# VectorE's order around the first item, the last expert's gather and last chunk, and a weight place that holds three chunks

## What is computed

```
logits = xt @ w_router + b_router            # 256 x 32
top_val, top_idx = top_k(logits, 4); gate = softmax(top_val)
for each expert e, for the tokens that chose it:
    hdn = x @ w_mlp1[e] + b_mlp1[e]          # 1024 -> 2048
    glu = min(hdn[:, :1024], 7); lin = clip(hdn[:, 1024:], -7, 7)
    y   = (glu * sigmoid(1.702 * glu) * (lin + 1)) @ w_mlp2[e] + b_mlp2[e]
out = sum over a token's 4 experts of gate * y
```

## Time and profile before

| what | value |
|---|---|
| median of three runs | 1119.99 us (1119.98 to 1119.99) |
| the profiled execution, its own time | 1121.66 us |
| its span, first to last instruction | 1119.8 us |
| mean granted TensorE clock | 0.995 |
| TensorE matmul busy | 1073.4 us (96%) |
| VectorE / ScalarE busy | 382.2 us (34%) / 247.1 us (22%) |
| read from HBM | 437.67 MB, 392 GB/s over the span |

### The profile page before, as it was taken

One profiled execution on the slowest core, in us unless ns is written; L12 is line 12 of the kernel. 1 busy time (PEld: TensorE's weight loads), 2 busy tenths in 40 slices (PEclk: granted clock), 3 DMA queues, 4 the chain that ended last, 5 costly groups with the idle time before them and its releaser, 6 DMA issues.

```text
span 1119.8 us, 14338 instructions
## 1 busy us (share of the span) xinstructions
PE 1073.4 (96%) x5327; PEld 471.7 (42%) x5328; DVE 382.2 (34%) x852; ACT 247.1 (22%) x346; POOL 3.0 (0%) x12
## 2 busy tenths in 40 slices
PE   8999999999999999999889999999988889998996
PEld 8888888533333333333333333333333333332332
DVE  5987787422232222222222222222222222222223
ACT  5745674311111111110111111111111111111112
POOL 0000000000000000000000000000000000000000
PEclk9999999999999999999999999999999999999999
DMA  9755488999999999999999999999999999999996
GB/s 331 238 164 170 154 273 363 424 419 422 428 427 434 429 431 434 430 429 431 431 433 404 432 431 431 431 431 431 431 431 431 433 431 434 434 433 433 423 424 265
DMA packets 38309, 439.15 MB, mean 392 GB/s; under 512 B 5292, under 2 KB 5480, under 8 KB 22440
## 3 DMA queue, kind: packets, MB, share of 16 engines
q1 hardware_dynamic: 37776, 437.26, 93.2%
q10 hardware_dynamic: 504, 1.47, 0.5%
HBM read 437.67 MB, written 1.05 MB: 392 GB/s over the span
## 4 chain that ended last, share of the span: by engine, by line
PE 70%; DMA 26%; DVE 2%; ACT 2%; issue 0%; DVEq 0%; SPq 0%; PEldq 0%; ACTq 0%
PE bank L1162 29%; PE bank L1217 15%; DMA late_slots<-in_w_mlp_dram 14%; DMA ring<-in_w_mlp_dram 11%; PE bank L821 9%; PE bank L1064 4%; PE bank L815 2%; PE bank L1103 2%; PE bank L983 2%; PE bank L1031 2%; PE bank L1087 1%; ACT xn L716 1%; PE bank L1154 1%; DMA xs<-in_x_dram 1%; PE bank L1080 0%
## 5 line engine op out<-in xcount | busy, mean ns | idle before, releaser
L1162 PE MATMUL bank<-ring,xn 128*64 128x512 f32 x1232 | 280.0, 602 | 18.3 <-DMA ring<-in_w_mlp_dram 18.2
L1162 PE MATMUL bank<-late_slots,xn 128*64 128x512 f32 x880 | 197.9, 596 | 12.6 <-DMA late_slots<-in_w_mlp_dram 12.6
L1162 PEld LDWEIGHTS bank<-ring,xn 128*64 128x64 f32 x1232 | 85.1, 138 | 179.5 <-issue 152.4
L1217 PE MATMUL bank<-ring,smo 128*64 128x512 f32 x624 | 138.3, 595 | 0.0
L728 ACT ACTIVATE xn<-bank 128x512 f32<-128x512 f32 x33 | 19.7, 598 | 436.6 <-PE bank L1162 436.6
L1162 PEld LDWEIGHTS bank<-late_slots,xn 128*64 128x64 f32 x880 | 59.9, 136 | 126.6 <-issue 105.4
L1730 DVE SCALAR_TENSOR_TENSOR moe_y_lo<-bank,st,moe_y_hi 128x512 fp32r<-128x512 f32 x33 | 24.8, 751 | 235.5 <-ACT moe_y_hi L735 235.5
L1217 PE MATMUL bank<-late_slots,smo 128*64 128x512 f32 x416 | 92.1, 595 | 0.0
L1714 DVE TENSOR_SCALAR xn<-xn 128x512 f32<-128x512 f32 x33 | 14.1, 427 | 190.8 <-ACT xn L728 190.8
L1217 PEld LDWEIGHTS bank<-ring,smo 128*64 128x64 f32 x624 | 43.0, 137 | 81.0 <-issue 81.0
L735 ACT ACTIVATE moe_y_hi<-bank,st 128x512 fp32r<-128x512 f32 x33 | 22.7, 688 | 243.2 <-PE bank L1217 243.2
(11 more groups left out here) (278 smaller groups left out, 871.8 us busy)
## 6 DMA issues: line engine op xcount, KB each, us to landing
ring<-in_w_mlp_dram SPq DMA_DIRECT2D x43, 4096.0 KB, 37.6
late_slots<-in_w_mlp_dram SPq DMA_DIRECT2D x29, 4096.0 KB, 35.5
ring<-in_w_mlp_dram SPq DMA_DIRECT2D x28, 2048.0 KB, 14.8
late_slots<-in_w_mlp_dram SPq DMA_DIRECT2D x14, 2048.0 KB, 16.3
ring<-in_w_in_dram SPq DMA_DIRECT2D x22, 1024.0 KB, 5.6
late_slots<-in_w_mlp_dram SPq DMA_DIRECT2D x8, 1024.0 KB, 35.5
ring<-in_w_branch_dram SPq DMA_DIRECT2D x4, 1024.0 KB, 5.0
ring<-in_w_out_dram SPq DMA_DIRECT2D x4, 1024.0 KB, 7.0
```

The costliest lines, as they stand in the source:

```text
L1162: last = mm(B[4 + u][g * C:(g + 1) * C, :], xgT[:, k % 4, k // 4, :], by_group(held[k // 2][0][:, k % 2, u * FF:(u + 1) * FF], g), start=F ...
L1217: last = mm(B[7][g * C:(g + 1) * C, :], actT[:, j, h * C:(h + 1) * C], held[4 + h][0][:, j // 2, (j % 2) * D + g * N:(j % 2) * D + (g + 1) ...
```

## The change

It is made of these edits:

- `ONCE = (5, 16, 27)`: the region `once` holds chunks 5, 16 and 27. Until chunk 27 is used there are 11 places, so chunk m + 11 is loaded when chunk m is free (m < 27), and m + 10 after that. SyncE's loads for experts 0 to 4's places are written out in a loop.
- `QUADS = range(6, 31)`: expert 30 too comes in transfers of 4 MB.
- The last expert's chunk 3 comes by columns: first piece the gated half's columns of both row blocks (1 MB in rows of 4 KB), then the linear half's columns of each row block (512 KB each). TensorE runs both gated products after the first piece.
- For the last expert `gather` stands between chunk 2 and chunk 3, and `turn_rows` between chunk 3 and the transposes.
- VectorE does gate3 and the first item's `own` and `turner` before item_expert; in its loop the next item's `own` and `turner` stand behind `ohT`'s copy.

```diff
-QUADS = range(ROUND + 1, E - 2)
+QUADS = range(ROUND + 1, E - 1)
+ONCE = (CHUNKS - 1, CHUNKS - 1 + PLACES + 1, CHUNKS - 1 + 2 * (PLACES + 1))
+EXTRA_LAST = ONCE[-1]
+def place_of(m):
+    return None if m in ONCE else (m - sum(o < m for o in ONCE)) % PLACES
...
-                if pieces == 2:
+                if pieces == 2 and i == 3:
+                    to, by = places[place], src.rearrange("p (a n) -> p a n", a=2)
+                    for rows_of, cut, done in ((slice(0, 2), slice(0, FF), place_landed[place]),
+                                               (slice(0, 1), slice(FF, SLOT), piece_landed[i]),
+                                               (slice(1, 2), slice(FF, SLOT), half_landed[i])):
+                        sp.dma_start(to[:, rows_of, cut], by[:, rows_of, cut]).then_inc(done, 16)
+                elif pieces == 2:
...
-            for i in range(CHUNKS - 1):
-                m = PLACES + 1 + i
-                if m != HALVED:
-                    wait_freed(after, i)
-                load(m // CHUNKS, m % CHUNKS, i)
...
+            for e in range((EXTRA_LAST + CHUNKS - 1) // CHUNKS):
+                after = sp.value_load(first_item[0:1, e + 1:e + 2], min_val=1, max_val=ITEMS - 1)
+                for i in range(CHUNKS):
+                    freed = CHUNKS * e + i
+                    m = freed + PLACES + (freed < EXTRA_LAST)
+                    if freed == EXTRA_LAST:
+                        continue
+                    if m // CHUNKS not in QUADS:
+                        if m != HALVED:
+                            wait_freed(after, i)
+                        load(m // CHUNKS, m % CHUNKS, place_of(m))
+                    elif m % 2:
+                        wait_freed(after, i)
+                        load_quad(m // CHUNKS, m % CHUNKS // 2, place_of(m - 1))
...
-            act.wait_ge(count_step, 9)
+            act.wait_ge(count_step, 14)
...
+                if last_expert:
+                    gather(2 * i + 4)
                 pe.wait_ge(held[3][1], held[3][2])
                 mlp1(KB - 2, 0)
+                mlp1(KB - 1, 0).then_inc(glu_done, 1)
                 if 3 in in_pieces:
                     pe.wait_ge(*in_pieces[3])
-                mlp1(KB - 1, 0).then_inc(glu_done, 1)
                 mlp1(KB - 2, 1)
                 if 3 in in_halves:
                     pe.wait_ge(*in_halves[3])
                 mlp1(KB - 1, 1).then_inc(slots_used, 2)
-                gather(2 * i + 4)
+                if last_expert:
+                    turn_rows(i + 2)
+                else:
+                    gather(2 * i + 4)
...
-                turn_rows(i + 2)
+                if not last_expert:
+                    turn_rows(i + 2)
...
+            own_of(cst[:, K_IOTA:K_IOTA + C], [pos[:, t, 0:1] for t in range(TT)], slice(0, 1))
             v.tensor_tensor(spread, cnt[:, 3, :].unsqueeze(1).broadcast_to([1, ITEMS, E]),
...
                 v.tensor_copy(ohT[:, :, :], B[7][:, 0:TT * wide].rearrange("p (t s) -> p t s", t=TT)[:, :, 0:P])\
                  .then_inc(gT_ready, 1)
+                own_of(places, at, bass.ds(after_this, 1))
```

More of the change, by code:

```diff
@@ L116, in landings @@
         e, i = m // CHUNKS, m % CHUNKS
-        if m == CHUNKS - 1:
-            table.append(None)
+        place = place_of(m)
+        if place is None:
+            table.append((None, ONCE.index(m) + 1))
             continue
-        place = m if m < CHUNKS else (m - 1) % PLACES
         if e in QUADS and i % 2:
@@ L1122, in chunks @@
             def chunks(e):
-                return [(places[(CHUNKS * e + i - 1) % PLACES], place_landed[landing[CHUNKS * e + i][0]],
-                         landing[CHUNKS * e + i][1] * 16) for i in range(CHUNKS)]
+                held = []
+                for m in range(CHUNKS * e, CHUNKS * (e + 1)):
+                    place, count = landing[m]
+                    held.append((once[:, :, :] if place is None else places[place_of(m)],
+                                 once_landed if place is None else place_landed[place], count * 16))
+                return held
             def chunks_in_round(c, r):
@@ L1140, in chunks_in_round @@
                             assert 0 < need <= past[-1]
-                    held.append((places[(CHUNKS * c + i - 1) % PLACES], place_landed[place],
+                    held.append((places[place_of(CHUNKS * (ROUND + c) + i)], place_landed[place],
                                  r * (16 * step) + 16 * (last - step * len(at))))
@@ L1147, in by_group, with item @@
                 return columns.rearrange("p (q g s) -> p g q s", g=2, s=ROWS)[:, g]
-            def item(i, held, in_pieces={}, in_halves={}):
+            def item(i, held, in_pieces={}, in_halves={}, last_expert=False):
                 pe.wait_ge(row_ready, i + 1)
@@ L1222, in _ @@
             with pe.Fori(0, after_first) as i:
-                item(i, [(places[n], place_landed[n], 16) for n in range(CHUNKS - 1)] + [(once[:, :, :], once_landed, 16)])
+                item(i, chunks(0))
             last_first = pe.value_load(first_item[0:1, E - 1:E], min_val=1, max_val=ITEMS - 1)
@@ L1670, in _, with own_of @@
             dve.wait_ge(mg_turned, 2 * TT)
[L1671 to L1678, removed]
             dve.wait_ge(firsts, 1)
             v.tensor_copy(gate3[:, :, :, 0], gate[:, :, :]).then_inc(count_step, 1)
+            dve.wait_ge(count_step, 8)
+            v.tensor_tensor(gate_rest[:, :, :], gate[:, :, :], gate3[:, :, :, 0], ALU.subtract).then_inc(count_step, 1)
+            dve.wait_ge(count_step, 9)
+            v.tensor_copy(gate3[:, :, :, 1], gate_rest[:, :, :]).then_inc(count_step, 1)
+            dve.wait_ge(count_step, 10)
+            v.tensor_tensor(gate_rest[:, :, :], gate_rest[:, :, :], gate3[:, :, :, 1], ALU.subtract).then_inc(count_step, 1)
             dve.wait_ge(count_step, 11)
-            v.tensor_tensor(gate_rest[:, :, :], gate[:, :, :], gate3[:, :, :, 0], ALU.subtract).then_inc(count_step, 1)
+            v.tensor_copy(gate3[:, :, :, 2], gate_rest[:, :, :]).then_inc(count_step, 1)
             dve.wait_ge(count_step, 12)
[L1684 to L1695, removed]
+            def own_of(places, at, e):
                 for t in range(TT):
```

25 lines of the change are left out of this document (18 added, 7 removed).

## The result

| | before | after |
|---|---|---|
| median (13 runs each, the same chip) | 1119.62 us (1118.76 to 1120.84) | 1121.76 us (1120.83 to 1123.65) |
| ratio to before, 95% interval | | 1.0019 (1.0012 to 1.0027) |
| the profiled execution, own time | 1121.66 us | 1123.65 us |
| mean granted TensorE clock | 0.995 | 0.994 |

The account below looks back on a forecast made before the run. The weight stream was taken to bound the steady part, TensorE's chain the end. Stream -1.8 and TensorE +2.4 + 0.35 gave +0.95 us, median 1120.9; own range 1120.3 to 1121.5, stated 8-in-10 range 1119.9 to 1122.8.

Parts of the forecast that it names:

- Expert 30 in 4 MB transfers: Tail: TensorE starts expert 30's third chunk 2.7 us later, expert 31's 2.4 us later; +2.4 in the sum.
- Gather in front: Last expert: second product 11.1 us after its third chunk's start T, against 10.76 measured before; +0.35 us.
- This gain reaches the end of the steady part whole, as TensorE hangs on landings there: -1.8: Stream near 250 us: the eleventh place has chunk 17 issued sooner, recovering 1.8 us lost between landings; bounds 0 and 1.8.
- VectorE's order: First item: TensorE's first turn_gates loses its 0.29 us wait, handed back at the next landing wait; 0 in the sum.
- rival A: Near 250 us: the early loss stays because a code transfer made chunk 17 late; 1122.7 us, chance 0.16.
- The cover that I named for the loop: VectorE's loop: own and turner, 1.3 us together, stand where VectorE waits for the sigmoid, so they cost 0.
- Rival B: Last experts: TensorE's clock falls after waits, 0.55 us at expert 30's first chunk, up to 1.7; 1121.5 to 1122.6, chance 0.12.
- Rival C: Tail: the end hangs on the stream after all, so the kernel gets faster, 1117.3 to 1118.0 us; chance 0.04.
- Rival D: Places and expert 30's transfers: both parts do nothing, since places are handed over as before; 1120.0 us, chance 0.03.

Follow-up runs that it names:

- after_again: The kernel after, unchanged, measured and profiled once more: 1122.04 us, ratio to before 1.0022.
- after_old_quads: The kernel after with expert 30 back in 2 MB transfers and the places' semaphores starting at 16: 1120.17 us, ratio to before 1.0001.
- after_plain_gather: The kernel after with the last expert's gather and turn_rows back where all experts have them, chunk 3 still by columns: 1120.79 us, ratio to before 1.0008.
- quads_only: The kernel before with only expert 30 in 4 MB transfers: 1121.44 us, ratio to before 1.0018.
- before_again: The kernel before, unchanged, measured and profiled once more: 1119.44 us, ratio to before 0.9999.
- dve_again: The kernel before with only VectorE's new order and ScalarE's wait for 14 steps, second run: 1119.09 us, ratio to before 0.9996.
- once_dve_cols: The kernel before plus the three-chunk place, VectorE's new order and chunk 3 by columns: 1118.49 us, ratio to before 0.9994.

## Why the prediction was right or wrong

**Expert 30 in 4 MB transfers: right.** Forecast +2.7 at its third chunk, +2.4 at expert 31's, relative to the stream; in after_again +2.72 and +2.35, with the forecast landing wait of 1.1 (1.14). Alone it costs 1.8 us.

**Gather in front: right.** Forecast T + 11.1, with 1.05 us against the plain order; measured 11.20 and 11.21, and 1.11 us in the rows (0.97 by the medians). Its purpose, to fill a wait for chunk 3, had no wait left to fill, since the edit beside it moved TensorE behind the landings. In after_old_quads, where that wait of some 0.7 us is left, the gather of 1.72 still puts the second product 0.43 later than in the kernel before: it is longer than what it was to fill.

**The step that failed: "This gain reaches the end of the steady part whole, as TensorE hangs on landings there: -1.8".** The mechanism was right up to 260 us, and the term was too large, for two reasons. The loss of 1.8 us was read from a single profile, and it is 0.6 to 1.0 in three others. And I followed the gain only to the next landing wait and not along the queue: at the two-item expert the stream runs dry in both kernels, and there the kernel after pays 1.6 us that the kernel before doesn't. Five of six such profiles pay there, one does not. By the medians what is left of the term is -0.65 us: after_plain_gather against quads_only, which differ in the place, VectorE's order and the columns. With that in place of -1.8 the sum is +2.4 + 0.35 - 0.65 = +2.1, the measured 2.1. This is no independent check, since the steps from before to quads_only (+1.82), after_plain_gather (-0.65) and after (+0.97) must add up to the measured 2.14. The -0.65 itself is not clear of noise, and the profiles don't show it: the stream of after_plain_gather is 0.4 longer than that of quads_only. That the -1.8 is not there is shown; whether a small gain or a small loss stands in its place is not.

The measured 1121.76 lies outside the forecast's own range of 1120.3 to 1121.5. It lies inside the stated one because rival A's price was added to that whole, and A did not happen: the hit is in part luck.

**VectorE's order: the term was right in its item and wrong behind it.** I said that 0.3 us is handed back at the next landing wait. It isn't handed back by then, because chunk 6 comes free within that item and the queue is about to run dry: 0.3 us sooner closes the whole early step. In the kernel after the place closes the same step, so only one of the two edits can count. The cover that I named for the loop held: the landing waits of the steady part are still 1.80, so an item of TensorE has not become longer.

**Rival A** (the early loss stays, 1122.7) named nearly the right price by the wrong mechanism: the step near 250 is gone, and a code transfer alone doesn't make it. One of 1.06 us lies at 249 to 251 in before_again, with a step 0.65 too long, in dve_again, with none, and in the kernel after, with none. The 1.88 us of the one in the kernel before may have added to its larger step; that isn't shown. The Trainium skill (Runtime: NRT & Kernel Launch, Instruction fetch mechanics) has the cost of a code fetch mostly hidden; the profile of the kernel after agrees at 251, where no step is missed. It is not the whole story of these profiles: one landing of the kernel after, at 405, comes 1.5 us late 8 us after a code transfer began, and one of the kernel before, at 456.6, 1.5 us late 7 us after one. Other code transfers have no such landing behind them, and no run tests it.

**Rival B**, the clock, happened in one profile and not in the other: 5.35 for 16 matmuls at 1057.66, 3.65 at 1058.27, after the same 1.80 of wait. In the first, expert 30's third chunk then came without a landing wait, and expert 31's lay 0.5 later relative to the stream (152.72 against 152.23); the forecast was 0.55. The Trainium skill (TensorE: Matmul & The Clock Gate, HAM oscillation) tells of a kernel with DMA waits of some 3 to 5 us in which every burst behind such a wait starts at the lower clock. The waits here are shorter, and the prediction read the page too widely when it made this the rule at each wait: in this profile of the kernel after, 2 of 12 waits of 1.30 to 1.81 ahead of a first chunk were followed by the lower level.

**Rival C** (the tail hangs on the stream) was not what happened, but the two versions without the costly edits end in just that state, at 1118.5 and 1118.9. **Rival D** is out, since chunks 16 and 17 are asked for sooner.

**What stays open.** Why the restart after the dry stretch is 1.1 to 1.7 us dearer with the three-chunk place. The issue times, the size and the absence of code transfers are the same; what differs is which place each chunk goes to, yet once_dve_cols, with the same places, doesn't show it. It was not tried to give those chunks other places. The trace narrows it: a transfer's landing is counted by 16 signals, one for each share of it. In the kernel after the last signal of the long step's transfer, at 610.6, comes 1.6 us behind the fifteenth; one transfer earlier it was 0.03 behind. In after_again it is 1.6 too, in after_old_quads 1.1, in once_dve_cols 0.1. So a single share is late, not the stream as a whole; why that one is, stays open.

## What to carry to other kernels

A gain in a stream counts only up to the next point at which its queue runs dry, so before it is carried to the end, look for the consumer's longest stop and count the distances between landings there. Larger transfers near the end trade stream time for grain: where the consumer is about to become the bound, each start is delayed to the end of a whole transfer, here 2.4 us for 0.2 us of stream (expert 30's six chunks take 29.15 us instead of 29.38). An edit that fills a wait is worth at most that wait, in the company that it will have: here the filling was 1.72 us and the wait 0.7, which cost 0.4, and where the edit beside it removed the wait it cost 1.1.

## What was not expected of the hardware

In window 598:600 of the kernel before the transfers fell to 98 GB/s and no landing came late. The landing signals of the 16 shares agree with this reading: the shares of a transfer don't run level, the last one sets the landing, and it has work left while the others are idle. The signals of the transfer that landed at 602.35 spread over 4.8 us, those of the next one, at 612.07, over 1.1. The shares that were ahead lost their lead, and the last one lost nothing. By this reading a dry stretch costs only what the last share stands still.

The lost step differs between executions of one kernel: near 250 us the kernel before lost 1.7 us in one profile and 0.65 in another, with chunk 17 asked for 10.9 and 9.7 us ahead of its landing. A term read from one profile at a place where a queue is just about to run dry needs a second profile.
